# Weight sums of five seven-product pairs by adding transfers, two factors in another order, swish in PSUM

## The reference, cut to what matters

```
def conv_ffn(h, w_up, conv_w, w_down):       # w_up 1024 x 5632, conv_w 3 x 5632
    gu = causal_dwconv(h @ w_up, conv_w)      # depthwise over tokens, 3 taps
    g, u = jnp.split(gu, 2, axis=-1)
    return (jax.nn.silu(g) * u) @ w_down
```

## Time and profile before

| | |
|---|---|
| device time, three runs | 1220.53, 1220.70, 1220.88 us (median 1220.7) |
| profiled execution, span of its instructions | 1219.1 us; its own device time is one of such executions, 1220.53 to 1220.88 |
| PE busy | 1201.6 us, 99% |
| DVE, ACT, POOL busy | 757.1, 630.4, 740.3 us |
| mean granted TensorE clock | 0.999 of full speed |
| DMA | 112.27 MB, mean 92 GB/s |

### The profile page before, as it was taken

The page is one execution under the profiler, slowest core; times in us unless marked ns, Lnnn a source line. Parts: engine busy times, 40 slices in busy tenths (PEclk is TensorE's granted clock), DMA queues, the critical chain, the costliest instruction groups (busy, mean ns, idle before and its releaser), DMA issues.

```text
span 1219.1 us, 18895 instructions
## 1 busy us (share of the span) xinstructions
PE 1201.6 (99%) x6847; PEld 993.6 (82%) x6847; DVE 757.1 (62%) x1305; ACT 630.4 (52%) x1220; POOL 740.3 (61%) x561
## 2 busy tenths in 40 slices
PE   8999999999999999999999999999999999999997
PEld 6987777777888899987887777878888888889886
DVE  6555426757646777745697555447888865966234
ACT  6365535676644344455644666546545454333544
POOL 8674232353269776855384566548878775886842
PEclk9999999999999999999999999999999999999999
DMA  7322222122223333354142223323323343333332
GB/s 238 104 89 84 66 61 61 52 69 71 70 64 102 95 98 94 106 180 117 52 115 60 56 65 93 98 69 95 96 78 109 92 122 86 96 96 117 109 87 70
DMA packets 62437, 112.27 MB, mean 92 GB/s; under 512 B 6856, under 2 KB 11464, under 8 KB 62344
## 3 DMA queue, kind: packets, MB, share of 16 engines
q1 hardware_dynamic: 62200, 111.06, 31.6%
q10 hardware_dynamic: 144, 0.00, 0.0%
HBM read 108.87 MB, written 2.16 MB: 91 GB/s over the span
## 4 chain that ended last, share of the span: by engine, by line
PE 89%; DVE 6%; ACT 1%; issue 1%; POOL 1%; DMA 0%; SPq 0%; DVEq 0%; ACTq 0%; POOLq 0%
PE pb L1143 21%; PE pb L1144 20%; PE pb L1146 20%; PE pb L1205 4%; PE pb L1207 4%; PE pb L1206 4%; PE pb L1361 2%; DVE cv L2059 2%; PE pb L1337 2%; PE pb L1214 2%; PE pb L1304 1%; PE pb L1275 1%; PE pb L1277 1%; PE pb L1276 1%; PE pb L1258 1%
## 5 line engine op out<-in xcount | busy, mean ns | idle before, releaser
L2793 POOL TENSOR_TENSOR wlo<-raw,whi 128x512 fp32r<-128x512 f32 (+3 forms) x379 | 522.5, 1397 | 323.1 <-ACT whi L1554 322.1
L1143 PE MATMUL pb<-HH,whi 128*128 128x512 f32 x776 | 313.9, 405 | 0.0
L1144 PE MATMUL pb<-HL,whi 128*128 128x512 f32 x776 | 306.8, 395 | 0.0
L1146 PE MATMUL pb<-HH,wlo 128*128 128x512 f32 x776 | 306.1, 394 | 0.0
L1554 ACT ACTIVATE whi<-raw 128x512 fp32r<-128x512 f32 (+3 forms) x379 | 224.4, 614 | 107.7 <-PE pb L1146 55.5
L1143 PEld LDWEIGHTS pb<-HH,whi 128*128 128x128 f32 x776 | 146.2, 188 | 38.2 <-issue 4.6
L1144 PEld LDWEIGHTS pb<-HL,whi 128*128 128x128 f32 x776 | 146.0, 188 | 34.4 <-issue 2.9
L1146 PEld LDWEIGHTS pb<-HH,wlo 128*128 128x128 f32 x776 | 145.9, 188 | 34.5 <-POOL wlo L2793 0.4
L1690 ACT ACTIVATE P<-P,stat 128x256 f32<-128x256 f32 (+3 forms) x96 | 50.5, 527 | 78.5 <-DVE stat L2352 56.0
L2059 DVE SCALAR_TENSOR_TENSOR cv<-pb,vecs,cv 128x511 f32<-128x511 f32 x88 | 65.5, 745 | 4.8 <-ACT cv L1954 3.2
L2047 DVE TENSOR_TENSOR pb<-pb,rff 128x512 f32<-128x512 f32 x44 | 30.1, 694 | 38.5 <-PE pb L1146 31.7
(11 more groups left out here) (480 smaller groups left out, 2791.4 us busy)
## 6 DMA issues: line engine op xcount, KB each, us to landing
raw<-in_wall SPq DMA_DIRECT2D x368, 256.0 KB, 2.7
raw<-in_wall SPq DMA_DIRECT2D x8, 260.0 KB, 2.9
X<-in_xT SPq DMA_DIRECT2D x8, 256.0 KB, 5.6
X<-in_xT SPq DMA_DIRECT2D x2, 1024.0 KB, 7.3
outT<-PP SPq DMA_DIRECT2D x8, 256.0 KB, 2.5
raw<-in_wall SPq DMA_DIRECT2D x10, 192.0 KB, 2.4
raw<-in_wall SPq DMA_DIRECT2D x9, 128.0 KB, 2.3
cst<-in_cst SPq DMA_DIRECT2D x1, 832.0 KB, 7.8
```

The source lines that it names most:

```text
L1143: pe.do.matmul(b, hi, xh[k], start=start, stop=False, skip_group_check=tile[0] == "down")
L1144: pe.do.matmul(b, hi, xl[k], start=False, stop=False, skip_group_check=tile[0] == "down")
L1146: m = pe.do.matmul(b, lo, xh[k], start=False, stop=stop, skip_group_check=tile[0] == "down")
L2793: g.do.tensor_tensor(lo, x, hi.bitcast(F32), ALU.subtract).then_inc(*up(name, point))
```

## The change

It does five things, all in the upward stage:

- S1, S3, S2 and S4 of the five upward pairs are made by transfers issued from POOL with an add at the destination, each 256 KB: A22 from DRAM onto the loaded A21 (S1), A21 from DRAM onto A11 (S3), A11 from DRAM onto S1 (S2), and S2 from SBUF onto A12 (S4). Only sums are made, so gate-half weights count with turned sign, and the combinations behind the products subtract where they added.
- A11, A21 and A12 of these pairs are loaded into three buffers of their own (the places of s7a, s8c, s7b) outside the ring of five.
- S1 and S2 change places. The lowerings of A22 and A12 go to DVE; POOL keeps five, that of S2 behind the issue of S4's transfer.
- U7 is copied in the step of S1 (when A11's product is done), and PE waits for it before S2. The steps of J-1 and J-2 move: scaled, taps 0, swish and product J-2 stand behind A11, taps 1 and product J-1 behind A22. The early split_to in front of the pair and the wider one behind S2 go.
- For all 22 j the tanh is written to the gate half's PSUM bank, and swish's product stays there; the bank is released by product, no longer by the last tap.

```diff
+UP_FACTORS = ("A11", "A22", "S1", "S2", "S3", "A12", "S4")
...
+        self.kept_at = {self.load_of[p, x]: i for p in range(NGATE, NUP) for i, x in enumerate(("A11", "A21", "A12"))}
+        self.ring_at, ring = {}, 0
+        for n in range(len(self.loads)):
+            if n not in self.kept_at:
+                self.ring_at[n] = ring
+                ring += 1
...
+        if step[0] == "product":
+            self.pending.discard(("ffn", 0, step[1]))
...
-        bank = min((b for b in range(8) if b not in self.kept), key=lambda b: self.held.get(b, -1))
+        bank = min((b for b in range(8) if b not in self.kept and self.holder.get(b) not in self.pending),
+                   key=lambda b: self.held.get(b, -1))
         self.hold(bank, tile)
+        if tile[:2] == ("ffn", 0):
+            self.pending.add(tile)
...
-        for x in FACTORS:
-            if not (NGATE <= p < NUP and x == "S2"):
-                self.split_to(self.unit_of[p, x] + LOOK)
+        for x in factors(p):
+            self.split_to(self.unit_of[p, x] + LOOK)
             self.add("product7", p, x)
-            if NGATE <= p < NUP and x == "S2":
+            if is_up(p) and x == "A11":
                 j = UPS[p - NGATE] - 1
-                self.split_to(self.unit_of[p, x] + NS)
                 self.add("scaled", 1, j)
                 self.add("taps", 0, j)
                 self.add("swish", j)
                 self.add("product", j - 1)
-            if x == "S3" and NGATE <= p < NUP:
+            if is_up(p) and x == "A22":
                 self.add("taps", 1, UPS[p - NGATE] - 1)
                 self.add("product", UPS[p - NGATE] - 1)
 
...
                 if half and j + 1 in UPS:
-                    self.split_to(self.unit_of[NGATE + UPS.index(j + 1), "S4"])
                     continue
...
+        KEPT = (S7["S1"], S8["S3"], S7["S2"])
+
+        def arrived(load):
+            n = int(plan.offset[load + 1] - plan.offset[load])
+            if load in plan.kept_at:
+                return KEPT[plan.kept_at[load]]
+            return raw[plan.ring_at[load] % NR][:, 0:n]
+
         def sums_at(p):
+            if is_up(p):
+                return {"S1": KEPT[1], "S2": KEPT[1], "S3": KEPT[0], "S4": KEPT[2]}
             return S7 if p < NGATE else S8
 
...
-                    elif x in ("A11", "S1", "A22"):
-                        free(tile)
+                    elif x == "S2":
+                        pe.wait_ge(*at("v0", p))
+                    else:
...
-                if kind(p) == "up" and x == "S2":
-                    a.wait_ge(*at("product7", p, x))
+                if kind(p) == "up" and x == "S1":
+                    a.wait_ge(*at("product7", p, "A11"))
                     a.wait_ge(*at("u3", p - 1))
                     a.do.activation(U7, ps("ffn", 0, UPS[p - NGATE])[:, 0:H], ACT.Copy).then_inc(*up("a_c7", ("v0", p)))
...
-                    a.wait_ge(*at("f_lo" if half else "product", j - 2))
+                    a.wait_ge(*at("f_lo" if half else "swish", j - 2))
...
             def swish(j):
                 a.wait_ge(*at("conv", 0, j))
-                if j >= 2:
-                    a.wait_ge(*at("swish", j - 2))
-                a.do.activation(cv[(3 * j + 1) % 6], cv[3 * j % 6], ACT.Tanh, scale=0.5).then_inc(
+                a.do.activation(ps("ffn", 0, j), cv[3 * j % 6], ACT.Tanh, scale=0.5).then_inc(
                     *up("a_gate", ("ffn_tanh", j)))
...
+                if is_up(p):
+                    if x in ("A22", "A12"):
+                        v.wait_ge(*at("raw", units[u][0]))
+                        v.wait_ge(*at("whi", u))
+                        v.do.tensor_tensor(wlo[u % NS][:, 0:T], arrived(units[u][0]), whi[u % NS][:, 0:T].bitcast(F32),
+                                           ALU.subtract).then_inc(*up("v_lo", ("wlo", u)))
...
+                again = p and p != NUP
...
-                def plus(dst, one, two, *points):
-                    v.do.tensor_tensor(dst, one, two, ALU.add).then_inc(*up("v_c7", *points))
+                def from_banks(dst, one, two, op, *points):
...
-                    plus(U7, ab[:, right], U7, ("u2", p))
...
-                    plus(W8, cd[:, left], U7)
-                    plus(ZU, cd[:, right], U7, ("u3", p))
+                    from_banks(W8, cd[:, left], U7, ALU.subtract)
+                    from_banks(ZU, cd[:, right], U7, ALU.add, ("u3", p))
                     v.wait_ge(*last("v_c7"))
-                    plus(e[:, right], cd[:, right], W8, ("empty", ("cd", j)))
-                    plus(e[:, left], e[:, left], ZU)
+                    from_banks(e[:, right], W8, cd[:, right], ALU.subtract, ("empty", ("cd", j)))
+                    from_banks(e[:, left], e[:, left], ZU, ALU.subtract)
                 elif x == "S4":
                     v.wait_ge(*at("product7", p, "S4"))
...
-                          *[("conv", half, j), ("empty", ("ffn", half, j))] * (i == 0), name="v_conv")
+                          *[("conv", half, j)] * (i == 0), *[("empty", ("ffn", 1, j))] * (half and i == 0),
+                          name="v_conv")
...
-                fused(g, cv[(3 * j + 1) % 6], 1.0, g, ALU.add, ALU.mult, ("swish", j), name="v_gate")
+                fused(b, b, 1.0, cv[3 * j % 6], ALU.add, ALU.mult, ("swish", j), name="v_gate")
...
-                fused(o, o, 0.5, cv[3 * j % 6], ALU.mult, ALU.mult, ("product", j), name="v_gate")
+                fused(o, o, 0.5, ps("ffn", 0, j), ALU.mult, ALU.mult, ("product", j), ("empty", ("ffn", 0, j)),
+                      name="v_gate")
...
+            def weights_added(p, x, to, source):
+                i = plan.kept_at[plan.load_of[p, to]]
+                g.do.dma_start(KEPT[i], source, accum_op=ALU.add).then_inc(
+                    *landing(f"landed_sum{i}", ("s7", p, x)))
+
+            def stored(p, x):
+                o = int(plan.offset[plan.load_of[p, x]])
+                return wall[:, o:o + T]
+
+            def split_up(u):
+                load, (p, x) = units[u]
+                if x in ("A11", "S1", "S3", "S2", "S4"):
+                    if load is not None:
+                        g.wait_ge(*at("raw", load))
+                        n = arrived(load)
+                    else:
+                        g.wait_ge(*at("s7", p, x))
+                        n = sums_at(p)[x]
+                    g.wait_ge(*at("whi", u))
+                    lower(wlo[u % NS][:, 0:T], n, whi[u % NS][:, 0:T], "wlo", ("wlo", u))
+                if x == "A11":
+                    g.wait_ge(*at("raw", plan.load_of[p, "A21"]))
+                    weights_added(p, "S1", "A21", stored(p, "A22"))
+                    g.wait_ge(*at("wlo", u))
+                    weights_added(p, "S3", "A11", stored(p, "A21"))
+                elif x == "S1":
+                    g.wait_ge(*at("wlo", u))
+                    weights_added(p, "S2", "A21", stored(p, "A11"))
...
+                if factor and is_up(factor[0]):
+                    p, x = factor
+                    if x == "S2":
+                        return
+                    if x == "A12":
+                        w = plan.unit_of[p, "S2"]
+                        g.wait_ge(*at("s7", p, "S2"))
+                        g.wait_ge(*at("wlo", u))
+                        weights_added(p, "S4", "A12", sums_at(p)["S2"])
+                        split_up(w)
+                        return
+                    split_up(u)
+                    return
...
+                    if is_up(p):
+                        freed[plan.load_of[p, "A21"]] = [("wlo", plan.unit_of[p, "S2"]), ("s7", p, "S4")]
+                        freed[plan.load_of[p, "A11"]] = [("wlo", plan.unit_of[p, "S3"])]
+                        freed[n] = [("wlo", plan.unit_of[p, "S4"])]
+                        continue
...
+                    weights = wall[:, int(plan.offset[n]):int(plan.offset[n + 1])]
+                    if n in plan.kept_at:
+                        i = plan.kept_at[n]
+                        p, x = next(y for y, m in plan.load_of.items() if m == n)
+                        earlier = plan.load_of[p - 1, x]
+                        if p > NGATE:
+                            for point in freed[earlier]:
+                                s.wait_ge(*at(*point))
+                        else:
+                            s.wait_ge(*at("full", ("wout", 7)))
+                            s.wait_ge(*at("wlo", plan.unit_of[p - 1, "S4"]))
+                        s.do.dma_start(arrived(n), weights).then_inc(*landing(f"landed_kept{i}", ("raw", n)))
+                        continue
+                    i = plan.ring_at[n]
+                    if i >= NR:
+                        for point in freed[in_ring[i - NR]]:
                             s.wait_ge(*at(*point))
-                    s.do.dma_start(raw[n % NR][:, 0:w], wall[:, int(plan.offset[n]):int(plan.offset[n + 1])]).then_inc(
-                        *landing(f"landed_raw{n % NR}", ("raw", n)))
```

(43 more changed lines are left out.)

20 lines of the change are left out of this document (9 added, 11 removed).

## The result

| | before | after |
|---|---|---|
| device time, median (runs) | 1220.62 us (4: 1219.22 to 1220.88) | **1269.26 us** (4: 1268.74 to 1271.09) |
| ratio, 95% interval | | 1.0403 [1.039, 1.0417] |
| span of the profiled execution | 1219.1 us | 1266.9 us |
| mean granted TensorE clock | 0.999 | 0.979 |

A forecast was written before the change was run, and what follows sets the result against it. PE, busy 99%, was taken as the bound, losing 5.0 us to late DVE in the upward stage. 1220.7 - 5.0 (relief) + 29.5 (U7 copy waits) + 6.8 (clock) = 1252.0 us, range 1236 to 1268.

The forecast's parts named there:

- DVE relief: Upward pairs: DVE's work falls by 4.9 us per 22.7 us, so the 5.0 us of PE waits go.
- The mechanism and its place: PE's S2, reached at t = 4.2 from a pair's first matmul, waits 5.9 us for ACT's U7 copy.
- the 27 us given as a sign: Sign that the forecast is right: pair starts some 27 us apart instead of 22.7.
- The chain behind the scaled step: Scaled, taps, swish and product (6.63 us), then ACT's FH, whi and U7 copy (1.47): 8.1 us in all.
- t_A = 2.0: DVE has lowered A12 and is free at 2.0 us after the pair's first matmul; the scaled step's chain follows.
- Five equal pairs: Each of the five upward pairs was given the same 5.9 us wait ahead of S2, 29.5 us in all.
- the wait term: PE's waits for U7's copy ahead of S2 in the upward pairs: 5 x 5.9 = 29.5 us.
- rival 3: Adding transfers land late, from 4.5 us up; beyond 3.9 each us costs two per pair: 1263 to 1286 us; chance 0.17.
- The clock, 6.8: TensorE's clock falls in four of five waits, each costing 1.7 us at half pace: 6.8 us.
- Rival 2: The S2 waits come at full clock, somewhat shorter, 4.1 to 5.9 us: 1236 to 1245 us; chance 0.2.
- The adding transfers' issue: POOL takes 1.0 us to issue each adding transfer, hidden because POOL loses two lowerings per pair (2.6 us).

## Why the prediction failed by 17 us, point by point

- **DVE relief, -5.0: right.** Those waits are gone in after, and swish in PSUM alone, with DVE's sums kept, gives 4.6 us. Swish and product took 0.70 and 0.69 us with one operand in PSUM, where 0.75 was taken from the earlier trace rows. The Trainium skill's rule on one and two SBUF inputs (SBUF — State Buffer, "Who interferes with whom") agrees with the trace: the swish took its 0.70 us beside a lowering of POOL's, while DVE's lowering of A12, with two SBUF inputs, took 1.33 us beside POOL's and 0.69 us with POOL idle. I had written that the relief came from the four sums above all; in the run, swish alone was enough.
- **The mechanism and its place: right.** All five waits are for U7's copy, at t = 4.2, and nothing else is in the list. The starts of pairs 3 to 5 stand 32.7, 30.5 and 30.8 us behind the ones before; the 27 us given as a sign was already too few for the prediction's own sum (20.88 + 5.9 + 1.7 = 28.5). The chain behind the scaled step was priced at 8.1 us and took 7.98.
- **t_A = 2.0: this step failed.** It took 3.55 us in pair 5, so the wait was 7.3 us where I had 5.9. I had put the landing of S2's sum and the roundings of S2 and S3 just ahead of A12's, done at -0.1. In the run S2's rounding alone began at 0.49. Of these 1.8 us (from -1.3), two landings of 4.2 instead of 3.7 make 1.0; a start 0.3 us later and the handovers that I left out (0.15 from the end of the rounding to POOL's lowering, 0.30 ahead of the issue) make the rest. The lowering of A12 beside POOL's took 1.33, not 1.10. Without S2's transfer t_A was 1.64 and the waits 27.1 us in all: the sum as written would have been near right, and what it had wrong is the time at which S2's sum is there.
- **Five equal pairs: this step failed too.** Pairs 1 and 2 waited 10.3 and 9.2 us, 5.3 us together above the later three's mean of 7.1. In pair 1 S1's transfer left at t = -7.4, 2.9 us later than in pair 5, and its sum had landed at -3.2; POOL was then busy with the lower halves of the transformed activations (2.99 us for two) and lowered it at 853.56, t = -2.2, so S2's sum was rounded at t = 3.57. Either was nearly enough by itself: without S1's transfer POOL lowered S1 at t = -2.2 as well. In pair 2 it left at t = -8.4, and S2's sum was rounded at 2.36. In both pairs POOL lowered A11, ahead of that issue, behind an `FL` and another lowering of the plain j before. I had taken the 5 of 20 us that POOL has free for cover, but a queue with the wrong instructions in front is no cover.
- **Together** the wait term was 41.0 us, not 29.5, and 27.1 without S2's transfer. That is rival 3's mechanism, which had 0.17, but not its size: its threshold of 3.9 us was passed by 0.3, worth 3 us by its own rule. The rest is the late start of the chain and the handovers in all pairs, and POOL's queue in pairs 1 and 2.
- **The clock, 6.8: mis-sized.** It fell behind all five waits, and each cost 2.0 to 2.65 us, not 1.7: 12.5. The granted clock was 0.50 for 5.3 us rather than the 3.56 of the earlier trace rows. Rival 2, the wait at full clock, rested on the clock's standing through waits of some 1 us; it did not come true behind any of the five.
- **The adding transfers' issue: right in size** (0.84 to 1.18 us, taken 1.0), but "hidden" was wrong, as it took no account of what is queued behind it. S4's transfer waits on POOL for DVE's lowering of A12 and holds S2's lowering behind it; under the copy's wait this was invisible in after. Once the copy was moved, PE waited 25 us for that lowering. The queue's order alone doesn't explain them, since turning it round gave nothing; with S2's transfer gone too, 4 us of these waits were left.

## What to carry to other kernels

When a copy or a sum moves ahead in a program with in-order queues, write down everything between its old and its new place on its engine, with the start of the chain at the earliest moment that its *last* input allows; a chain of transfers, roundings and lowerings that has two tenths of a microsecond to spare has no cover. Before moving work from a full engine, try the smallest edit that relieves it: here an operand in PSUM took away all the waits of the stage. And count a wait of an otherwise full TensorE with the half-speed stretch that follows it.

## What the runs showed of the hardware

- An adding transfer of 256 KB from DRAM to SBUF landed in 4.2 us in after (3.9 to 4.5 in all kernels, but for two of 5.8 and 6.1), where a plain one took 2.7, and one from SBUF to SBUF in 3.6. S3's transfer, issued 0.6 us behind S1's, took 5.7 us in after; where S1's transfer was left out or stood far ahead, the same transfer took 4.0 to 4.3 us, but for two of 4.8 and 5.0. POOL was busy with the issue of each for 0.84 to 1.18 us in after.
- The clock falls after much shorter waits than I had read from the earlier trace rows, and not after each. Busy time and granted clock of the kernel with neither the late copy nor S2's transfer, behind a wait of 1.14 us (pair 4) and behind one of 2.03 (pair 5):

```profile
945.00:950.00 5.00, 4.98 (x33) 4.62 (x34) 3.25 (x7) 3.53 (x8) 4.63 (x5) 1.00 0.39 103
965.60:970.60 5.00, 5.00 (x29) 5.00 (x30) 4.46 (x9) 2.40 (x6) 3.03 (x3) 0.66 0.12 22
```

  and the same of the kernel with the early copy and the early S1, behind a wait of 2.62 us (pair 2) and behind one of 2.70 (pair 5):

```profile
903.70:907.40 3.70, 2.96 (x24) 2.76 (x24) 3.60 (x6) 1.52 (x3) 2.45 (x2) 1.00 0.46 106
...
980.60:985.60 5.00, 4.99 (x30) 5.00 (x31) 4.22 (x8) 2.59 (x5) 3.27 (x3) 0.69 0.12 23
```

  Where it fell, a wait of 2.0 us cost 1.7 more at half speed, and one of 7 to 10 us cost 2.0 to 2.65: nearly a fixed fee. Why two waits of like length differ stays open.
- Filling the waits with 56 useless matmuls each gave back 9 us of the 12.5 at half speed: the kernel with more work for PE was 9 us faster.
